# Empty tiles of 32 to 96 bytes between the ring slots of the split weights and ahead of the activations

## What is computed

```python
def reference(x, ...):
    for i in range(DEPTH):                      # DEPTH = 2
        xn = _rmsnorm(x, norm_gain[i])
        if i % 2 == 0:
            y = _diff_attention(xn, ...)        # xn @ w_in (2048 x 8192), 8 heads, then @ w_out (2048 x 2048)
        else:
            y = _conformer_conv(xn, ...)        # xn @ w_in (2048 x 6144), 31 taps, layer norm, then @ w_out
        x = x + y
    return _rmsnorm(x, final_gain)
```

## Time and profile before

| | |
|---|---|
| median of 3 runs | 851.56 us (851.52 to 852.56) |
| profiled execution | 852.14 us |
| its span in the profile | 850.4 us |
| mean granted clock of TensorE | 0.999 |
| PE busy | 842.2 us, 99% of the span |
| DVE busy | 646.2 us, 76% |
| ACT busy | 449.0 us, 53% |
| POOL busy | 220.2 us, 26% |
| DMA, mean share of 16 engines | 193 GB/s over the span |

### The profile page before, as it was taken

How to read it: one execution, slowest core, us unless ns; L and a number is a source line. 1 busy time by engine, 2 the same in 40 slices (tenths; PEclk the granted TensorE clock), 3 DMA queues, 4 the chain that set the end, 5 groups by cost and what they waited for, 6 DMA issues and landing times.

```text
span 850.4 us, 13797 instructions
## 1 busy us (share of the span) xinstructions
PE 842.2 (99%) x5630; PEld 769.5 (90%) x5630; DVE 646.2 (76%) x1093; ACT 449.0 (53%) x586; POOL 220.2 (26%) x75
## 2 busy tenths in 40 slices
PE   9999999999999999999999999999999999999996
PEld 9998899889998899888888899999999999988885
DVE  6569784697658784698788978999999998566651
ACT  7756543546346543556544365455554556594432
POOL 0000000000000000002000008888888887680000
PEclk9999999999999999999999999999999999999999
DMA  9977556545554556534655565555555555549502
GB/s 326 395 278 252 167 190 207 175 141 198 200 194 148 166 190 208 177 120 153 232 181 186 189 207 183 175 180 199 180 177 190 191 179 185 191 151 343 196 3 99
DMA packets 99089, 163.74 MB, mean 193 GB/s; under 512 B 3504, under 2 KB 39600, under 8 KB 98520
## 3 DMA queue, kind: packets, MB, share of 16 engines
q1 hardware_dynamic: 97408, 160.50, 55.7%
q10 hardware_dynamic: 1624, 2.45, 0.8%
HBM read 160.83 MB, written 3.69 MB: 193 GB/s over the span
## 4 chain that ended last, share of the span: by engine, by line
PE 97%; SPq 1%; DMA 1%; ACT 0%; DVE 0%; issue 0%
PE ps_acc L1205 17%; PE ps_acc L1208 17%; PE ps_acc L1207 17%; PE ps_acc L1194 14%; PE ps_acc L1191 14%; PE ps_acc L1193 14%; DMA sb_w_raw<-in_attn_w_in 1%; SPq L320 0%; PE ps_a L1296 0%; PE ps_a L1295 0%; PE ps_d L1282 0%; PE ps_d L1281 0%; PE ps_a L1294 0%; PE ps_d L1280 0%; PE ps_a L1165 0%; SPq L322 0%
## 5 line engine op out<-in xcount | busy, mean ns | idle before, releaser
L432 ACT ACTIVATE sb_w_hi<-sb_w_raw 128x2048 fp32r<-128x2048 f32 x140 | 267.1, 1914 | 253.3 <-PE ps_acc L1208 171.7
L404 POOL TENSOR_TENSOR sb_w_lo<-sb_w_raw,sb_w_hi 128x2048 fp32r<-128x2048 f32 x45 | 208.5, 4637 | 435.0 <-ACT sb_w_hi L432 435.0
L777 DVE TENSOR_TENSOR sb_w_lo<-sb_w_raw,sb_w_hi 128x2048 fp32r<-128x2048 f32 x95 | 216.2, 2289 | 103.5 <-ACT sb_w_hi L432 103.1
L1205 PE MATMUL ps_acc<-sb_conv_hi,sb_w_hi 128*128 128x256 f32 x768 | 215.0, 280 | 0.0
L1208 PE MATMUL ps_acc<-sb_conv_hi,sb_w_lo 128*128 128x256 f32 x768 | 213.8, 278 | 0.0
L1207 PE MATMUL ps_acc<-sb_conv_lo,sb_w_hi 128*128 128x256 f32 x768 | 213.7, 278 | 0.0
L1007 DVE SCALAR_TENSOR_TENSOR ps_d<-sb_uT,sb_dwT,ps_d 128x256 f32<-128x256 f32 x480 | 188.9, 482 | 4.5 <-ACT ps_d L659 4.5
L1191 PE MATMUL ps_acc<-sb_w_hi,sb_act_hi 128*128 128x512 f32 x384 | 151.4, 394 | 0.0
L1193 PE MATMUL ps_acc<-sb_w_lo,sb_act_hi 128*128 128x512 f32 x384 | 151.3, 394 | 0.0
L1194 PE MATMUL ps_acc<-sb_w_hi,sb_act_lo 128*128 128x512 f32 x384 | 151.3, 394 | 0.0
L1208 PEld LDWEIGHTS ps_acc<-sb_conv_hi,sb_w_lo 128*128 128x128 f32 x768 | 144.2, 188 | 0.0
(11 more groups left out here) (169 smaller groups left out, 841.3 us busy)
## 6 DMA issues: line engine op xcount, KB each, us to landing
sb_w_raw<-in_attn_w_in SPq DMA_DIRECT2D x60, 1024.0 KB, 5.4
sb_w_raw<-in_conv_w_in SPq DMA_DIRECT2D x64, 512.0 KB, 4.5
sb_w_raw<-in_attn_w_out SPq DMA_DIRECT2D x16, 1024.0 KB, 5.0
sb_w_raw<-in_conv_w_in SPq DMA_DIRECT2D x16, 1024.0 KB, 5.2
sb_w_raw<-in_conv_w_out SPq DMA_DIRECT2D x16, 1024.0 KB, 5.0
sb_w_raw<-in_attn_w_in SPq DMA_DIRECT2D x4, 512.0 KB, 7.8
sb_xs<-in_x SPq DMA_DIRECT2D x2, 1024.0 KB, 15.6
sb_w_raw<-in_attn_w_in SPq DMA_DIRECT2D x7, 256.0 KB, 5.4
```

Source lines behind the costliest of these rows:

```text
L404: pool.tensor_tensor(w_lo[c % RING][:], w_raw[c % RING][:], w_hi[c % RING][:].bitcast(F32), ALU.subtract).then_inc(lo_ready_pool, 1)
L432: act.activation(w_hi[slot][:], w_raw[slot][:], ACT.Copy).then_inc(hi_ready, 1)
L777: dve.tensor_tensor(w_lo[slot][:], w_raw[slot][:], w_hi[slot][:].bitcast(F32), ALU.subtract).then_inc(lo_ready, 1)
L1205: pe.matmul(into, left_hi, hi[:, kt], start=(kt == 0 and f % 2 == 0), stop=False, skip_group_check=True)
```

## The change

A tile that nothing reads or writes is placed behind each slot of `w_hi` and of `w_lo`, of 8, 16, 16 and 24 floats (32, 64, 64 and 96 bytes), one of 16 floats (64 bytes) ahead of `act_hi`, and one of 64 bytes ahead of `conv_hi`. `w_raw` stays where it is. No instruction is added, removed or moved on any engine.

```diff
+SLOT_GAPS = (8, 16, 16, 24)
+ACT_GAP, CONV_GAP = 16, 16
...
-        w_hi = [sb(f"w_hi{i}", [P, CK, GW], F32R) for i in range(RING)]
-        w_lo = [sb(f"w_lo{i}", [P, CK, GW], F32R) for i in range(RING)]
+        def slots(name):
+
+            tiles = []
+            for i in range(RING):
+                tiles.append(sb(f"{name}{i}", [P, CK, GW], F32R))
+                sb(f"gap_{name}{i}", [P, SLOT_GAPS[i]])
+            return tiles
+
+        w_hi, w_lo = slots("w_hi"), slots("w_lo")
...
         with ExitStack() as one:
+            sb("gap_act", [P, ACT_GAP], F32, one)
             act_hi = sb("act_hi", [P, KT, SEQ], F32R, one)
...
             with ExitStack() as two:
+                sb("gap_conv", [P, CONV_GAP], F32, two)
                 conv_hi = sb("conv_hi", [P, KT, SEQ], F32R, two)
```

## The result

The changed kernel takes 855.69 us (median of 6 runs, 855.31 to 856.6) against 851.91 us for the kernel before on the same chips: ratio 1.0047, 95% interval 1.0037 to 1.0057. The forecast was 839.2 us, in a range of 824 to 861. The time lies in the range, on the wrong side of no change.

The account below looks back on a forecast made before the run. The prediction took PE's matmul pace to bound the kernel. Its terms, -13.7 us for 256-column matmuls and +1.3 us of returned wait, summed to -12.4 us, giving 839.2 us at the median, in a range of 824 to 861.

Parts of the forecast that it names:

- What bounds the kernel: Whole kernel: PE is busy 99% of the span, so time is the number of matmuls times PE's pace.
- What the change can touch: Matmuls of 256 columns: paces of 113.3, 117.8 and 120.0 ns, with 120.0 going with operand starts at distance 0 modulo 256 bytes.
- The picture of two reads that meet: While a matmul streams its moving operand, the next one's weights are read; the reads meet or not by distance and phase.
- Cost 1: 256-column matmuls of attention and convolution: 64 slow chunks all reach 113.3 ns, -13.7 us; worst end +11.3 us.
- the sign of a wrong step: 256-column chunks in attention and convolution: pace differing by slot with some at 117.8 or 120, or falling below 113.3.
- Cost 2: Convolution, ahead of PE's last transposes: DVE can't follow a faster PE fully, so 1.3 us comes back as PE wait.
- Cost 3: The 1,536 matmuls of 512 columns: pace stays 233.3 ns, zero change; ends -30.7 and +10.2 us.
- the rival: 512-column matmuls gain too: one step less on each is -10.2 us, around 829 us; chance 0.21.
- Cost 4: Scores, probabilities x values, head, tail and the splits by ACT, DVE and POOL: zero change.
- odd starts: Slots 1 to 3, 512-column matmuls: starts 32 bytes off a multiple of 64 cost +7.7 us, 859.3; chance 0.19.
- Distances 32 and 224 act as 0 does: 256-column chunks lose their fast phases and run at 120 ns: +11.3 us, 862.9; chance 0.11.
- Nothing happens: Whole kernel: pace is set by phase alone, not by operand starts; 851.6 us; chance 0.13.

## Why the prediction was wrong, step by step

- **What bounds the kernel:** right. PE's pace is the time, before and after. PE's waits grew by 0.6 us and the busy times of DVE, ACT and POOL moved by 0.6 us at most.
- **What the change can touch:** right in the main. Of one shape of matmul there are several paces, the distance has a say in which of them comes, and distance 0 costs 120.0. The runs with one distance throughout showed it: 120.0 at 0, 113.3 at 112. The picture of two reads that meet fits with this and was not shown. One reading ahead of the sum was short: a slow stretch of the kernel before holds not for 100 to 250 matmuls but for up to 479, from 498.25 to 554.66 us.
- **Cost 1, the turned chunks, "I take the fast pace":** this step failed. It took -13.7 us and the traces show +3.9. Its three reasons: that no new distance is 0 was no help, since 96 costs as much as 0. Being further from 0 or 256 than 64 was no measure either, since 32 (116.7) is faster than 96 (120.0) and 128 (118.7). And "a slow phase should not last" was wrong because at the new distances there is mostly no fast pace to fall into: at 32, 96, 128, 160 and 224 no run showed 113.3, and at 192, which has it, half of the chunks were slow. What came is what the prediction named as the sign of a wrong step: paces that differ by slot, some at 117.8 or 120. The price was bounded by rows of three paces, and the true mean lies inside those bounds (118.4 ns in the attention, 117.8 in the convolution); choosing the best end was not earned by any row. That 855.69 lies in the stated range is no merit of the mechanism: the range ran from one rival's gain to another's loss, and no case of the prediction gave 855.
- **Cost 2, DVE's 1.3 us:** did not come up in the changed kernel. With distance 112 the turned chunks did run at 113.3, and PE showed no wait at the last transposes: ACT's copy ended at 706.61 and PE turned at 706.97, so the slack shrank from 1.0 to 0.4 us, and DVE no longer waited for PE in that stretch. The term was 1.3 and measured 0 there.
- **Cost 3, the straight matmuls at zero:** right for this change (-0.1 us in all, slot means by stage between 231.3 and 234.2), for a reason that doesn't hold in general: their pace does follow the distance, 226.7 to 234.4 in the table, but these distances give next to nothing. The output products at distance 0 got the 6.7 ns a matmul that the rival named.
- **Cost 4:** right; scores and probabilities x values took 119.6 ns on average against 119.2, +0.1 us in all.
- **The rivals:** odd starts fell by the run with both operands 32 bytes later. "Distances 32 and 224 act as 0 does" fell too, at 116.7 and 118.3, though its direction was right: other distances, 96 and in part 160, took that place, and the fast phases were lost. "Nothing happens" fell: the starts of the tiles alone move the pace between 113.3 and 130 ns with nothing else at work. The Trainium skill's rule in "TensorE: Matmul & The Clock Gate", section "Step-by-step: what each phase is for", says that loading the next weights takes no read bandwidth from the running matmul. By it, the prediction said, the distance couldn't matter, and that does not fit with these runs. Whether the rule itself is wrong they don't tell, since it was not shown which reads meet.

## What to carry to other kernels

Where PE is busy all the time and matmuls of one shape show more than one pace, measure the pace against the distance of the two operands' starts in a kernel that does nothing else, over one period and in the order of the real one, and only then place the tiles; then read the pace in the kernel itself, since 128 gave 118.7 ns alone and 120.0 in most of the attention. One good distance for every slot did better here than a spread of distances, which takes about the mean of good and bad. And a pace that depends on how a stretch begins is worth less than an equal one that doesn't: 192 and 112 promise the same 113.3 for the turned chunks, and only 112 kept it.

## What the runs showed of the hardware that was not expected

- A period of 256 bytes in the distance of the two operands, with paces of 113.3 to 120.1 ns for 256 columns at multiples of 16 bytes and 226.7 to 234.7 for 512, and up to 129.8 at a distance of 104.
- Two steady paces at the same starts, 113.3 and 117.8 at 64 and at 192, kept for hundreds of matmuls. With nothing else at work the length of the interruption before chose between them. At 128 (118.5 and 120.0) and 160 (117.4 and 120.0) there is more than one pace too; what chooses there was not shown, but at 160 it went with the pace of the slot before.
- Moving both operands by 32 bytes left the time as it was (851.82 us, ratio 0.9999). At distance 112, got by moving the weights by 144 bytes in place of the activations by 112, the pace was 120.0 and not 113.3.
- The two forms want different distances: 0 is among the worst for the turned form (120.0) and among the best for the straight one (226.7).
